# Input and up projections as seven block products per pair of units, unpadded tokens, gates through DRAM

## What is computed

```python
h = rms_norm(x, norm1_g)
z = h @ w_in                       # 1024 -> 4608
a_val, a_gate, b_g, c_g, b_val, gates = split(z)
u = a_val * sigmoid(a_gate)
u, new_a = causal_dwconv(u, st_a, dw_a)          # 31 taps, 512 channels
u = silu(layer_norm(u + b_dw_a, ln_a_g, ln_a_b))
y_a = u @ w_a_out
v, new_b = causal_dwconv(c_g * b_val, st_b, dw_b)  # 3 taps
y_b = (b_g * v) @ w_b_out
g_a, g_b = split(sigmoid(gates + b_gate))
x = x + (g_a * y_a + g_b * y_b) @ w_o
h = rms_norm(x, norm2_g)
f_gate, f_val = split(h @ w_up)                  # 1024 -> 2 x 2816
f_gate, new_f = causal_dwconv(f_gate, st_f, dw_f)  # 3 taps
x = x + (silu(f_gate) * f_val) @ w_down
y = rms_norm(x, final_g)
```

## Time and profile before

| | |
|---|---|
| median of 3 runs | 1481.09 us (1480.67 to 1481.42) |
| profiled execution, first to last instruction | 1479.4 us |
| TensorE busy | 1456.1 us, 8774 matmuls |
| VectorE busy | 781.2 us |
| ScalarE busy | 308.7 us |
| GpSimd busy | 26.4 us |
| HBM read, written | 72.04 MB, 4.63 MB |

### The profile page before, as it was taken

The page is one execution under the profiler, slowest core; times in us unless marked ns, Lnnn a source line. Parts: engine busy times, 40 slices in busy tenths (PEclk is TensorE's granted clock), DMA queues, the critical chain, the costliest instruction groups (busy, mean ns, idle before and its releaser), DMA issues.

```text
span 1479.4 us, 20930 instructions
## 1 busy us (share of the span) xinstructions
PE 1456.1 (98%) x8774; PEld 1448.6 (98%) x8774; DVE 781.2 (53%) x744; ACT 308.7 (21%) x329; POOL 26.4 (2%) x57
## 2 busy tenths in 40 slices
PE   6999999999999999999999999999999999999997
PEld 6999999999999999999999999999999999999997
DVE  5575888755642225346635363545454535354545
ACT  5321111111252214134111111111111111101012
POOL 3000000000000000000000000000000000000001
PEclk9999999999999999999999999999999999999999
DMA  5111111111022222112202020201010101010103
GB/s 188 53 43 43 43 43 43 41 45 43 29 72 71 71 71 64 43 43 72 72 15 71 14 71 14 71 26 59 28 57 28 57 28 57 28 57 29 61 2 121
DMA packets 107898, 77.18 MB, mean 52 GB/s; under 512 B 2469, under 2 KB 101527, under 8 KB 107863
## 3 DMA queue, kind: packets, MB, share of 16 engines
q1 hardware_dynamic: 106631, 72.22, 15.6%
q10 hardware_dynamic: 1232, 4.46, 0.9%
HBM read 72.04 MB, written 4.63 MB: 52 GB/s over the span
## 4 chain that ended last, share of the span: by engine, by line
PE 98%; DVE 1%; DMA 0%; POOL 0%; ACT 0%; issue 0%; DVEq 0%; SPq 0%
PE X L400 48%; PE Y L400 47%; PE S L562 1%; DMA xr<-in_x_prompt 0%; PE S L510 0%; PE Y L455 0%; DVE out_rows L1336 0%; PE S L668 0%; PE S L528 0%; PE Y L668 0%; POOL stats L377 0%; PE S L455 0%; DVE h_lo L957 0%; ACT h_hi L717 0%; DVE res L1345 0%
## 5 line engine op out<-in xcount | busy, mean ns | idle before, releaser
L400 PE MATMUL X<-h_hi,w_hi 128*128 128x364 f32 (+1 forms) x1056 | 347.7, 329 | 2.6 <-issue 2.4
L400 PE MATMUL X<-h_lo,w_hi 128*128 128x364 f32 (+1 forms) x1056 | 348.3, 330 | 0.0
L400 PE MATMUL Y<-h_lo,w_hi 128*128 128x364 f32 (+3 forms) x1056 | 347.6, 329 | 0.0
L400 PE MATMUL Y<-h_hi,w_hi 128*128 128x364 f32 (+3 forms) x1056 | 347.3, 329 | 0.0
L400 PE MATMUL X<-h_hi,w_lo 128*128 128x364 f32 (+1 forms) x1056 | 346.9, 329 | 0.0
L400 PE MATMUL Y<-h_hi,w_lo 128*128 128x364 f32 (+3 forms) x1056 | 346.3, 328 | 0.0
L957 DVE TENSOR_TENSOR w_lo<-w_raw,w_hi 128x1024 fp32r<-128x1024 f32 (+1 forms) x104 | 118.7, 1142 | 415.5 <-ACT w_hi L704 415.5
L704 ACT ACTIVATE w_hi<-w_raw 128x1024 fp32r<-128x1024 f32 (+1 forms) x104 | 103.2, 993 | 798.7 <-PE Y L400 485.9
L400 PEld LDWEIGHTS X<-h_hi,w_hi 128*128 128x128 f32 x1056 | 199.1, 189 | 3.4 <-issue 2.8
L400 PEld LDWEIGHTS Y<-h_hi,w_hi 128*128 128x128 f32 x1056 | 198.5, 188 | 0.6 <-issue 0.5
L400 PEld LDWEIGHTS X<-h_hi,w_lo 128*128 128x128 f32 x1056 | 199.0, 188 | 0.0
(11 more groups left out here) (166 smaller groups left out, 1380.4 us busy)
## 6 DMA issues: line engine op xcount, KB each, us to landing
w_raw<-in_w_up SPq DMA_DIRECT2D x44, 512.0 KB, 3.7
w_raw<-in_w_in SPq DMA_DIRECT2D x36, 512.0 KB, 3.7
mid<-in_w_down SPq DMA_DIRECT2D x11, 1024.0 KB, 5.9
xr<-in_x_prompt SPq DMA_DIRECT2D x8, 512.0 KB, 3.8
xr<-in_x_prompt ACTq DMA_DIRECT2D x8, 512.0 KB, 4.3
w_raw<-in_w_o SPq DMA_DIRECT2D x8, 512.0 KB, 3.4
out_y_prompt<-out_rows SPq DMA_DIRECT2D x8, 512.0 KB
w_raw<-in_w_b_out SPq DMA_DIRECT2D x8, 256.0 KB, 2.6
```

Source lines behind the costliest of these rows:

```text
L400: done = pe.matmul(dst, w, act[:, k, cols[0]:cols[1]], start=(first and p == 0), stop=(last and p == 2))
```

## The change

Tokens are kept without pads, T = 1088, in two halves of 544 (PW), each of two quarters of 272 columns (HP). Input and up projections are done as 2 x 2 block products after Strassen: the 1024 input channels are four pairs of k tiles (an even and an odd tile), the tokens of a half are two quarters, and two output units are made together. The even k tiles of weights of unit 1 and 2 are A11 and A21, the odd ones A12 and A22; the activation blocks are B11, B12 (even tiles, quarters 1 and 2) and B21, B22. Seven products replace eight: of A11, S1 = A21 + A22, S2 = S1 + A11, S4 = S2 + A12, S3 = A11 + A21, A12 and A22 with activation sums prepared once (T1N, T2N, T3, T4; `hb` holds seven blocks of each tile pair in high and low part). 43 *jobs* do this: A (gate and value of mixer A), B (two of its three operands), G (third operand, two channel slices), S (merge gates), F (FFN gate and value). A job over both halves is 7 x 2 x 4 x 3 = 168 matmuls of 272 columns; four A jobs and the first F pair are cut into one job for each half.

What the other engines get for it:

- GpSimd: `weight_sums` (4 sums of 512 columns a job), `block_sums` (4 sums and a negation of 272 columns for each of 16 tile pairs), `c22_sum` (544 columns a job), the sums of the layer norm over channels, the merge additions, the sums of squares.
- ScalarE: `copies`, four bank copies a job (after products 0, 1, 2 and 4), weight splits of 512 columns three products ahead (`hi`), the evacuation of the transposed x, the high parts of `hb`, all 12 parameter loads at its queue's start, and the stores of the merge gates to DRAM (16 rows of 557 KB), which SP loads back in P1 and P2.
- VectorE: `c12_sum`, `c11_sum`, low parts, products with the third sums out of PSUM, and the 124 taps by a table `TAPS`.
- All merge gates are made before P1; P1 and P2 are then 8 units each, halves in a ring of three bank pairs; w_o runs half after half; the residual's x loads move to the SP queue. The last down group waits for its whole input, and runs half after half.
- No hardware loops: every program is written out.

The core of the diff (lines left out where "..." stands):

```diff
+    BOTH, FIRST, SECOND = slice(0, 2), slice(0, 1), slice(1, 2)
+    JOBS = [("A", 0, FIRST), ("A", 1, FIRST), ("A", 0, SECOND), ("A", 1, SECOND), ("A", 2, BOTH), ("A", 3, BOTH)]
+    JOBS += [("B", c, BOTH) for c in range(KB)] + [("G", i, BOTH) for i in range(KB // 2)]
+    JOBS += [("S", i, BOTH) for i in range(KD)]
+    J_B, J_G, J_S, J_F = 6, 10, 12, 20
+    JOBS += [("F", 0, FIRST), ("F", 0, SECOND)] + [("F", f, BOTH) for f in range(1, KF)]
...
+            def three(dst, w, at, hi, lo, first, last):
+                pe.matmul(dst, w_hi[:, w, at:at + P], hi, start=first, stop=False, skip_group_check=True)
+                pe.matmul(dst, w_hi[:, w, at:at + P], lo, start=False, stop=False, skip_group_check=True)
+                return pe.matmul(dst, w_lo[:, w, at:at + P], hi, start=False, stop=last, skip_group_check=True)
...
+            def product(j, s, bank, blk, first, ready=None):
+                n, ps = BASE[j] + s, JOBS[j][2]
+                pe.wait_ge(wlo, n + 1)
+                for p in range(ps.start, ps.stop):
+                    for k in range(KJ):
+                        if ready:
+                            ready(p, k)
+                        at = (HB_W if j < J_F else HB_F)[p][k]
+                        last = three(bank[:, p, 0:HP], n % RING, k * P, hb[:, at, 0, blk, :], hb[:, at, 1, blk, :],
+                                     first and k == 0, k == KJ - 1)
+                last.then_inc(used, 1)
...
+            def job(j, after=()):
+                x, y = x_bank(j), y_bank(j)
+                kind, f, ps = JOBS[j]
+                g = (f - 3) // 2 if kind == "F" and f % 2 and f >= 3 else None
+                if j == 0:
+                    pe.wait_ge(hn, KD)
+                elif j == J_F:
+                    pe.wait_ge(wo_added, 15)
+                else:
+                    pe.wait_ge(c11, j)
+                    if g is not None:
+                        pe.wait_ge(down_added, 16 * g + 14)
+                product(j, 0, x, B11, True, blocks_ready(j, 0))
+                hook(after, 0)
+                if j == J_F:
+                    pe.wait_ge(wo_added, 16)
+                elif j:
+                    pe.wait_ge(c12, j)
+                    if g is not None:
+                        pe.wait_ge(down_added, 16 * g + 15)
+                product(j, 1, BC, T1N, True, blocks_ready(j, 1))
+                hook(after, 1)
+                pe.wait_ge(cp, 4 * j + 1)
+                product(j, 2, x, T2N, False, blocks_ready(j, 2))
+                hook(after, 2)
+                pe.wait_ge(cp, 4 * j + 2)
+                product(j, 3, BC, B22, False, blocks_ready(j, 3))
+                hook(after, 3)
+                pe.wait_ge(cp, 4 * j + 3)
+                product(j, 4, x, T3, False, blocks_ready(j, 4))
+                hook(after, 4)
+                if j and j != J_F:
+                    pe.wait_ge(*x_free(j - 1))
+                product(j, 5, y, B21, True, blocks_ready(j, 5))
+                hook(after, 5)
+                pe.wait_ge(cp, 4 * j + 4)
+                product(j, 6, x, T4, False, blocks_ready(j, 6))
+                hook(after, 6)
...
+            job(0, [lambda k=k: turn_x(1, k) for k in range(7)])
+            job(1, [lambda: turn_x(1, 7)])
+            for j in range(2, J_F - 1):
+                job(j)
+            job(J_F - 1, [None, lambda: mean_part(0), None, None, lambda: mean_part(1)])
...
+            def hi(n):
+                if n >= N_END:
+                    return
+                if n >= RING:
+                    act.wait_ge(used, n - RING + 1)
+                if n in DIRECT:
+                    act.wait_ge(w_in[n % RING], DIRECT[n])
+                    src = w_raw[:, n % RING, :]
+                else:
+                    j = max(j for j in range(len(BASE)) if BASE[j] <= n)
+                    s = n - BASE[j]
+                    src = stg[:, (A11, S1, S2, S4, S3, A12, A22 + j % 2)[s], :]
+                    if s == 0:
+                        act.wait_ge(a11_in, 16 * (j + 1))
+                    elif s == 5:
+                        act.wait_ge(a12_in, 16 * (j + 1))
+                    elif s == 6:
+                        act.wait_ge(a22_in[j % 2], 16 * (j // 2 + 1))
+                    else:
+                        act.wait_ge(sums, 4 * j + (0, 2, 3, 4, 1)[s])
...
+            def copies(j, s):
+                ps = JOBS[j][2]
+                kind = JOBS[j][0]
+                if s == 1:
+                    act.wait_ge(used, BASE[j] + 1)
+                    if kind == "A" and j >= 2:
...
+                    act.activation(unit1(j, 0), x_bank(j)[:, ps, 0:HP], ACT.Copy).then_inc(cp, 1)
...
+        TAPS = {4: 9, 5: 9, 6: 6, 7: 6, 8: 6, 9: 6, 10: 8, 11: 8, 12: 10, 13: 10, 14: 10, 15: 9, 16: 9, 17: 9, 18: 9}
...
+            blocks_b_lo(2)
+            blocks_t_lo(0)
+            normalise(6)
+            blocks_b_lo(3)
+            blocks_t_lo(1)
+            lo(2)
+            normalise(7)
+            blocks_t_lo(2)
+            normalise(8)
+            blocks_t_lo(3)
+            normalise(9)
...
+            def c12_sum(j):
+                ps = JOBS[j][2]
+                dve.wait_ge(cp, 4 * j + 3)
+                dve.wait_ge(used, BASE[j] + 4)
+                dst = ss23(j) if JOBS[j][0] in "GF" else unit1(j, 1)
+                dve.tensor_tensor(dst, BC[:, ps, 0:HP], ss23(j), ALU.add).then_inc(c12, 1)
+            def c11_sum(j):
+                dve.wait_ge(used, BASE[j] + 6)
+                dve.tensor_tensor(unit1(j, 0), y_bank(j)[:, JOBS[j][2], 0:HP], unit1(j, 0), ALU.add).then_inc(c11, 1)
...
+                    if s == 4:
+                        c12_sum(j)
+                        if kind == "G":
+                            b_gate(j, 0, 1)
+                    elif s == 6:
+                        c11_sum(j)
+                    taps(quota)
...
+                        dve.wait_ge(mean_out, 2)
+                        for c in range(KA):
+                            dve.wait_ge(tap_done, KA * TAPS_A)
+                            dve.tensor_tensor(cv[c][:, :], cv[c][:, :], sq_b[:, :], ALU.subtract).then_inc(centred, 1)
...
+            def weight_sums(j):
+                pool.wait_ge(a11_in, 16 * (j + 1))
+                pool.wait_ge(a21_in, 16 * (j + 1))
+                if j:
+                    pool.wait_ge(wlo, BASE[j - 1] + 5)
+                pool.tensor_tensor(stg[:, S3, :], stg[:, A11, :], stg[:, A21, :], ALU.add).then_inc(sums, 1)
+                pool.wait_ge(a22_in[j % 2], 16 * (j // 2 + 1))
+                pool.wait_ge(sums, 4 * j + 1)
+                pool.tensor_tensor(stg[:, S1, :], stg[:, A21, :], stg[:, A22 + j % 2, :], ALU.add).then_inc(sums, 1)
+                pool.wait_ge(sums, 4 * j + 2)
+                pool.tensor_tensor(stg[:, S2, :], stg[:, S1, :], stg[:, A11, :], ALU.add).then_inc(sums, 1)
+                pool.wait_ge(a12_in, 16 * (j + 1))
+                pool.wait_ge(sums, 4 * j + 3)
+                pool.tensor_tensor(stg[:, S4, :], stg[:, S2, :], stg[:, A12, :], ALU.add).then_inc(sums, 1)
...
+            def block_sums(v):
+                x, y = hn_of(v), ts_of(v)
+                b11, b12, b21, b22 = x[:, 0, 0:HP], x[:, 0, HP:PW], x[:, 1, 0:HP], x[:, 1, HP:PW]
+                pool.wait_ge(hn, 2 * v + 2)
+                if v >= 2:
+                    pool.wait_ge(t_lo, v - 1)
+                pool.tensor_tensor(y[:, T1N, :], b11, b12, ALU.subtract).then_inc(tsum, 1)
+                pool.tensor_tensor(y[:, T3, :], b22, b12, ALU.subtract).then_inc(tsum, 1)
+                pool.wait_ge(tsum, 5 * v + 2)
+                pool.tensor_tensor(y[:, T2N, :], b11, y[:, T3, :], ALU.add).then_inc(tsum, 1)
+                pool.wait_ge(tsum, 5 * v + 3)
+                pool.tensor_tensor(y[:, T4, :], y[:, T2N, :], b21, ALU.subtract).then_inc(tsum, 1)
+                pool.wait_ge(tsum, 5 * v + 4)
+                pool.tensor_scalar(y[:, T2N, :], y[:, T2N, :], -1.0, None, ALU.mult).then_inc(tsum, 1)
...
+            for j in range(1, J_F):
+                if 1 < j < J_F - 1:
+                    weight_sums(j + 1)
+                c22_sum(j)
...
+            def gate_row(i):
+                if i < 4:
+                    sp.wait_ge(used, N_P1)
+                else:
+                    sp.wait_ge(gated, 2 * (i - 4) + 2)
+                k = i // 2
+                s = 2 * (k % 2) + i % 2
+                sp.wait_ge(spilled[s], 16 * (k // 2 + 1))
+                sp.dma_start(gates[:, i % 4, :], spill[i, :, :]).then_inc(gate_in[i % 4], 16)
```

2452 lines of the change are left out of this document (1389 added, 1063 removed).

## The result

The changed kernel takes 1678.4 us (median of 4 runs, 1677.4 to 1681.8) against 1480.9 before (1480.7 to 1481.4): a ratio of 1.134, 95% interval 1.132 to 1.135, **13.4% slower**. The forecast was 1446, in a range of 1400 to 1488. The profiled execution has a span of 1680.0.

The account below looks back on a forecast made before the run. TensorE, 98% busy, was taken as the bound: 1291 us stream, 51 start, 18 other TensorE work, 10 + 12 + 12 seams, 15 tail and 2 first G job make 1411; 33 lock and 1.7 around the span give 1446, range 1400 to 1488.

Parts of the forecast that it names:

- a dearer step (0.136): Every product: weight load paces TensorE at 272 columns, 0.136 us a matmul, 119 us more, 1565; chance 0.11.
- N/2.4 + 2.5 ns: Every product: a matmul of N columns takes this time, 90 us less in all, 1356; chance 0.04.
- The lock: Jobs' taps and weight splits: VectorE waits while GpSimd sums, 33 us; the forecast case, 1446, chance 0.45.
- Plain weights ring: 0: SP queue: residual rows behind weights and gate rows, whose ring waits end four earlier than needed, cost 0.
- P1 and P2: 0: P1 and P2: 3.0 us a half against a 0.64 multiply and a 1.0 sum, so no loss.
- WO to FFN 12 (6 to 18): Seam from w_o to FFN: ScalarE's preparation of units and GpSimd's queued weight sums cost 12 us.
- The start, 51: Start through jobs 0 and 1: first product near 29, one product by 42, ScalarE and GpSimd pacing; 51 us (44 to 62).
- Cold steps, 2 in each of two seams: Before P1 and before the last down group: TensorE at 1.2 GHz after an idle stretch, 2 us each.
- Seam to P1 10: Last job to P1: mean row, subtractions and splits before the products, 8 us plus 2 for cold steps.
- end 12: After the last job's c11: serial chain of taps, silu, scale, value steps and split, 10 us plus 2 cold.
- tail 15: After the last product: five output tiles where three were, with squares, root, norm and last store, 15 us.
- Rival 4: Start and seams cost half again as much by GpSimd queueing and 1.2 GHz steps: 20 to 55 more, near 1485; chance 0.14.

Follow-up runs that it names:

- one exchange of lines: Changed kernel with GpSimd making a tile pair's block sums before adding the next row's square, second half of w_o: 1656.3 us.
- the three orders: Changed kernel with c22 in q_raw and q split later, block sums ahead of squares, first w_down load ahead of the last w_up: 1593.8 us.

## Why the prediction was wrong

The sum was 236 us short of the profiled span: 98 in the FFN pairs, 52 in the second half of w_o with F0 and F1, 36 at the start, 25 in P1 and P2, 21 in jobs 4 to 18, 4 elsewhere.

- **The stream: right.** 0.125 a step, 1291 us; the rivals of a dearer step (0.136) and of N/2.4 + 2.5 ns fall. The constant price per column carried to a width seen in no row. The prediction held N/2.4 + 2.5 ns of the Trainium skill (TensorE: Matmul & The Clock Gate, Back-to-back issue gap) against the trace as if it were meant for a stream; that section gives it for an isolated matmul and says that a stream of weight loads and matmuls keeps another pace, so the trace and the section don't disagree there.
- **The lock: right in kind, too small, and priced in one stage only.** The term mis-sized is GpSimd's sum. With no VectorE instruction beside it, it takes 1.28 for 512 columns and 1.35 for 544, 6.5 a job, not 5.0. By the prediction's own step, 4.3/5.0 of that, each of 14 jobs pays 1.3 more: 33 + 18 = 51. The run with narrow weight sums gave 46. That the two are so near is partly luck: the added sums cost 20 us for an estimated 32 of sum (30 of 1.08, by the line through the 0.76 for 272 columns and the 1.28 for 512), 0.62 of each us and not 0.86. My estimate of 1.12, scaled from the 2048 columns of the Trainium skill (GPSIMD Engine Reference, Elementwise — side-by-side cycle accounting), was nearer than 1.0; by the same step it gives 41, not the 38 that the prediction says. What was missed is that the FFN pays it too, about 5 us a pair in the order of this kernel.
- **"FFN: two jobs and one down group are 66 us of TensorE against about 43 of VectorE. Hidden."** This is the step that failed, 98 us: busy times were added up to a cover, and the waits in the queues were put at nothing. VectorE is busy 50 of 75 us there, so it has room to spare, and TensorE waits all the same. A copy stood behind a wait on a buffer, that behind a value step, two scalings, a silu and three taps: it starts 12.7 us after the job's first matmul, in a job whose fourth product could start after 9. The question to ask was what each of the four bank copies of a job has ahead of it in ScalarE's queue.
- **"Plain weights ring: 0" and "P1 and P2: 0".** 49 us by the run without loads. A load that starts only when its slot is given back is in time for TensorE, but the engine that waits for it in order also carries the copies; and the SP queue that issues it stood at another wait. In P1 the row of the layer norm adds to it: VectorE's step stands behind a split that waits for a load, and the gap ahead of the eighth half is 7.7 us with loads and 3.8 without, 2.8 of it the row's own matmuls.
- **"WO to FFN 12 (6 to 18)": 64 for both parts of it**, of which 19 were the ring of waits that one exchange of lines took away. The list of what each engine does was right; in which order GpSimd does it I didn't follow.
- **The start, 51: 87.** "hn 8 near 29" left out that the fifth and the seventh evacuation wait for block sums, as two slots hold the rows; the sums of the first pair stand behind four weight sums, and the first product came at 38.9. The block sums are 16.6 of these 87 by their run. The second product, forecast at 42, came at 55.3: the transposes in TensorE's queue ahead of it wait for the tenth normalised tile, and the power that this tile needs ends at 54.25 on GpSimd, behind the block sums of four tile pairs.
- **Cold steps, 2 in each of two seams: 66 in all.** The rule was in the prediction ("an idle stretch of 7 to 10 us will cost such steps again"). Stalls of 4.4 us do it as well, and there is one in every pair; the run with matmuls in the stall shows that price by itself. The prediction put the term at 4 for the seams and at nothing for the FFN.
- **Seam to P1 10, end 12, tail 15: 10.0, 14.4, 16.5.** The first two forecasts held 2 each for cold steps, so the bare chains were 8 and 10; the agreement of 10 with 10.0 is partly luck. Without plain loads the same two gaps are 7.2 and 11.6: the chains that were written out step by step came out within 2 us, and the load that each of them left out was 2.8. Those that were called hidden did not come out.
- **Rival 4**, with its queueing and its 1.2 GHz between bursts, named the right kind of mechanism, at 0.14, but at the start and the seams only, and capped at 55 us. No rival looked at the steady FFN pairs. The lock and the queues can't be parted into two sums: with the weight sums nearly gone the kernel is 110 us faster, with the three orders 85, with both 150 of the 197 that it is slower than before.

What stays open: how much of the start and of F0 and F1 an order could win back, since the runs took sums away there, not waits; and why the run with fills is 7 us below the changed kernel.

## What to carry to other kernels

When a change spreads work over more engines, a busy share below one proves nothing: for each wait of the bounding engine, list what stands ahead of the releasing instruction in its queue, and what that waits for, buffers and loads included, and compare its time with the time at which the bounding engine comes. Being a few us late in such chains cost here 98 us in the FFN pairs alone, of the 122 that the stream had saved; a stall of 4.4 us brought with it 3.6 us at a granted clock of 0.55. Price a new kind of instruction from a run if there is no row for it, and add its lock wherever the two engines overlap, not only where one is full.

## What was not expected of the hardware

- VectorE steps with two SBUF operands and GpSimd sums out of SBUF hold each other up, both ways and in turn. The forecast took this for the taps; what it costs was not known: 64 columns took 1.28 us beside a sum and 0.22 without, 1024 columns 2.23 and 1.22. At the start a scaling with one SBUF operand is stretched too (0.75 alone, 1.24 to 1.25 beside sums). Few VectorE steps out of PSUM overlap a sum, and those are not stretched: three of 544 columns take 0.71 to 0.73, five of 272 take 0.43. GpSimd fills (0.53 for 512 columns) delay nothing.
- GpSimd's two-operand sum alone: 0.76 us for 272 columns, 1.28 for 512, 1.35 for 544.
- TensorE's granted clock behind a stall of 4.4 us: 0.55 for 3.6 us. Thirty matmuls in the stall whose result nobody uses kept it at 1.00, and made the kernel 13 us faster.
